# HGRN scores of a two-layer decoder: one array per block size, and the four heads scored in one stretch

## The reference, cut to what matters

```python
# hq, hf, hi: (256, 4 heads, 128) slices of h @ w_in
log_f = log(lb + (1 - lb) * sigmoid(hf));  k = (1 - lb) * sigmoid(-hf);  q = silu(hq)
b = cumsum(log_f over t)
scores[t, s] = sum_d q[t, d] * exp(b[t, d] - b[s, d]) * k[s, d]   for s <= t, else 0
o = scores @ hi * 128 ** -0.5
```

## Time and profile before

| | |
|---|---|
| median of 3 runs | 1288.95 us (1288.56 to 1290.48) |
| the profiled execution | 1287.09 us, of it 1285.1 us span |
| busy: PE, PEld, DVE, ACT, POOL | 993.1, 433.0, 243.0, 153.8, 12.6 us |
| chain that ended last | DMA 48%, PE 42%, SP's queue 4%, DVE 3% |
| mean granted TensorE clock | 0.872 of 2.4 GHz |

### The profile page before, as it was taken

One profiled execution on the slowest core, in us unless ns is written; L12 is line 12 of the kernel. 1 busy time (PEld: TensorE's weight loads), 2 busy tenths in 40 slices (PEclk: granted clock), 3 DMA queues, 4 the chain that ended last, 5 costly groups with the idle time before them and its releaser, 6 DMA issues.

```text
span 1285.1 us, 12164 instructions
## 1 busy us (share of the span) xinstructions
PE 993.1 (77%) x5148; PEld 433.0 (34%) x5148; DVE 243.0 (19%) x668; ACT 153.8 (12%) x320; POOL 12.6 (1%) x12
## 2 busy tenths in 40 slices
PE   5999998986767776766759987997776867767765
PEld 5657645421212121212227544542212312121211
DVE  3410225111101000101030564331101101000101
ACT  3523311100000000000021222110000000000000
POOL 0000001000000000000000000100000000000000
PEclk9988899987879878878789998998877878778878
DMA  7963067899999999999997413869999999999995
GB/s 248 302 248 131 14 279 296 341 429 427 428 429 426 429 426 429 427 428 428 417 392 255 149 69 148 340 280 430 427 428 427 428 427 428 427 429 426 429 421 218
DMA packets 62150, 448.53 MB, mean 349 GB/s; under 512 B 13072, under 2 KB 13328, under 8 KB 39568
## 3 DMA queue, kind: packets, MB, share of 16 engines
q1 hardware_dynamic: 62096, 447.73, 84.5%
HBM read 446.66 MB, written 1.05 MB: 348 GB/s over the span
## 4 chain that ended last, share of the span: by engine, by line
DMA 48%; PE 42%; SPq 4%; DVE 3%; ACT 1%; issue 1%; DVEq 0%; ACTq 0%
PE psum L519 17%; DMA ring<-in_w_up 14%; PE psum L741 11%; DMA ring<-in_w_down 10%; DMA wide<-in_w_gate 10%; DMA wide<-in_w_down 9%; DMA ring<-in_w_gate 5%; PE psum L783 5%; PE psum L736 2%; SPq L384 2%; SPq L328 1%; PE psum L475 1%; PE psum L836 1%; PE psum L482 1%; PE psum L838 1%
## 5 line engine op out<-in xcount | busy, mean ns | idle before, releaser
L519 PE MATMUL psum<-ring,mixed 128*32 128x512 f32 x1664 | 406.5, 714 | 123.8 <-DMA ring<-in_w_up 54.2
L519 PE MATMUL psum<-wide,mixed 128*32 128x512 f32 x1408 | 401.4, 710 | 108.8 <-DMA wide<-in_w_gate 62.4
L519 PEld LDWEIGHTS psum<-ring,mixed 128*32 128x32 f32 x1664 | 93.0, 128 | 328.1 <-issue 162.0
L519 PEld LDWEIGHTS psum<-wide,mixed 128*32 128x32 f32 x1408 | 88.6, 127 | 274.1 <-issue 123.2
L741 PE MATMUL psum<-ring,wide 128*128 128x512 f32 x320 | 145.5, 613 | 0.6 <-DMA ring<-in_w_in_ab 0.6
L741 PEld LDWEIGHTS psum<-ring,wide 128*128 128x128 f32 x320 | 62.3, 198 | 76.9 <-issue 75.8
L623 DVE TENSOR_TENSOR mixed<-psum,sig 128x512 f32<-128x512 f32 x16 | 16.9, 1056 | 277.9 <-PE psum L519 277.9
L482 PE MATMUL psum<-y_sb,spread 128*128 128x512 f32 x144 | 66.6, 605 | 1.6 <-DVE y_sb L628 1.6
L475 PE MATMUL psum<-sel,h 128*128 128x128 f32 x520 | 64.4, 283 | 3.5 <-DVE sel L596 3.5
L475 PEld LDWEIGHTS psum<-sel,h 128*128 128x128 f32 x520 | 61.0, 196 | 17.1 <-issue 13.4
L783 PE MATMUL psum<-ring,wide 128*128 128x512 f32 x128 | 58.7, 618 | 6.1 <-ACT wide L712 3.5
(11 more groups left out here) (238 smaller groups left out, 529.9 us busy)
## 6 DMA issues: line engine op xcount, KB each, us to landing
ring<-in_w_down SPq DMA_DIRECT2D x38, 2048.0 KB, 35.1
ring<-in_w_up SPq DMA_DIRECT2D x36, 2048.0 KB, 37.7
wide<-in_w_gate SPq DMA_DIRECT2D x34, 2048.0 KB, 36.6
ring<-in_w_gate SPq DMA_DIRECT2D x30, 2048.0 KB, 30.9
wide<-in_w_up SPq DMA_DIRECT2D x28, 2048.0 KB, 28.5
wide<-in_w_down SPq DMA_DIRECT2D x26, 2048.0 KB, 34.7
ring<-in_w_in_ab SPq DMA_DIRECT2D x8, 2048.0 KB, 16.6
ring<-in_w_in_cd SPq DMA_DIRECT2D x6, 2048.0 KB, 21.4
```

Of the source, the lines that this page charges most:

```text
L519: mm = pe.matmul(psum[slots, out + n, :], inp[:, c, slots], slot(layer, unit)[:, at + 512 * n:at + 512 * (n + 1)], start=c == 0, stop=c == ...
```

## The change

Per head, the score matrix is now made in five parts. The **near part** covers pairs within one block of 16: queries and keys referred to the middle of their own block, two matmuls of 128 x 128 (one for each half of the sequence; what lies outside the diagonal blocks is overwritten, or masked). Then for each **block size** 16, 32, 64, 128 one array `x_level` holds in its even blocks the keys and in its odd blocks the queries, both referred to the border between the two. One matmul per pair of blocks gives their rectangle: 8, 4, 2 and 1 matmuls with 16, 32, 64 and 128 stationary and moving columns. That is 17 matmuls a head.

ACT makes the factors with six exponentials of 128 x 1024 for all heads at once, in place of 96 short ones, and no longer takes the log of the keys. DVE makes the differences (eight subtractions of 128 x 512) and the products (two of 128 x 1024, eight of 128 x 512). POOL's two memsets go. As no array is reused, all four heads are scored behind projection 3. The masks of HGRN come before the second rotation, and the router's scaling, with its wait for the small tables, comes behind all masks. The two tables of constants get a semaphore of their own; the order of SP's DMAs stays. The new arrays lie in `h`, `wide` and `y_sb`.

```diff
             def scores_hgrn(hd):
-                pe.wait_ge(S["qe_ready"], 1)
-                pe.wait_ge(S["ke_ready"], hd + 1)
+                pe.wait_ge(S["near_ready"], 1)
                 bank = next_scores()
-                for i in range(NSUB):
-                    q = q2T[:, hd, i * SUB:(i + 1) * SUB]
-                    mm = pe.matmul(psum[:, bank, i * SUB:(i + 1) * SUB], ke0[:, i, :], q, start=True, stop=True)
...
+                for lo in range(0, SEQ, P):
+                    pe.matmul(psum[:, bank, at(lo):at(lo) + P], near_k[:, hd, lo:lo + P], near_q[:, hd, lo:lo + P],
+                              start=True, stop=True, skip_group_check=True)
+                pe.wait_ge(S["levels_ready"], len(LEVELS))
+                for width, x_level in reversed(list(zip(LEVELS, levels))):
+                    for lo in range(0, SEQ, 2 * width):
+                        mid = lo + width
+                        cols = at(mid) if width < P else P
+                        mm = pe.matmul(psum[lo % P:lo % P + width, bank, cols:cols + width], x_level[:, hd, lo:mid],
+                                       x_level[:, hd, mid:mid + width], start=True, stop=True, skip_group_check=True)
...
             for n in range(4):
                 project(0, n)
-            scores_hgrn(0)
+            for hd in range(HEADS):
+                scores_hgrn(hd)
             pe.wait_ge(S["roped"], 1)
             turn_roped(0)
             project(0, 4)
-            scores_hgrn(1)
...
             project(0, 5)
-            scores_hgrn(2)
...
-            scores_hgrn(3)
             project(0, 6)
...
             nc.scalar.activation(tmp, tmp, ACT.Ln).then_inc(S["f_log"], 1)
-            nc.scalar.activation(flat(k2T), flat(k2T), ACT.Ln).then_inc(S["f_log"], 1)
+            act.wait_ge(S["mid_in"], 1)
+            nc.scalar.activation(flat(near_k), tmp, ACT.Exp, scale=-1.0)
+            nc.scalar.activation(flat(near_q), tmp, ACT.Exp).then_inc(S["mid_exp"], 1)
+            for i, x_level in enumerate(levels):
+                act.wait_ge(S["level_in"], i + 1)
+                nc.scalar.activation(flat(x_level), flat(x_level), ACT.Exp).then_inc(S["level_exp"], 1)
             wait_projected(act, 2)
             nc.scalar.activation(flat(q2T), flat(proj(1)), ACT.Sigmoid).then_inc(S["q_sig"], 1)
...
-            dve.wait_ge(S["small_landed"], 16 * N_SMALL)
+            dve.wait_ge(S["consts_landed"], 32)
...
+            for width, x_level in zip(LEVELS, levels):
+                keys, queries = sides(cumf, width)
+                key_part, query_part = sides(x_level, width)
+                border = keys[:, :, width - 1].unsqueeze(2).broadcast_to([P, HEADS * SEQ // (2 * width), width])
+                V.tensor_tensor(key_part, border, keys, ALU.subtract)
+                V.tensor_tensor(query_part, queries, border, ALU.subtract).then_inc(S["level_in"], 1)
             dve.wait_ge(S["q_sig"], 1)
             and_wait(dve, V.tensor_tensor(flat(q2T), flat(proj(1)), flat(q2T), ALU.mult), proj_used[1], 1)
             dve.wait_ge(S["mid_exp"], 1)
+            V.tensor_tensor(flat(near_k), flat(near_k), flat(k2T), ALU.mult)
+            V.tensor_tensor(flat(near_q), flat(near_q), flat(q2T), ALU.mult).then_inc(S["near_ready"], 1)
+            for i, (width, x_level) in enumerate(zip(LEVELS, levels)):
+                dve.wait_ge(S["level_exp"], i + 1)
+                for dst, src in zip(sides(x_level, width), (sides(k2T, width)[0], sides(q2T, width)[1])):
+                    r = V.tensor_tensor(dst, dst, src, ALU.mult)
+                r.then_inc(S["levels_ready"], 1)
```

More of the change, by code:

```diff
@@ L35 @@
 NSUB = SEQ // SUB
+LEVELS = (16, 32, 64, 128)
 N_GROUPS = 4
@@ L46 @@
 KEPT_CONSTS = FIRST_CONSTS + 2 * P + SEQ + 32 + N_EXPERTS
-N_SMALL = 21
+N_SMALL = 19
 RING = 6
@@ L68 @@
 F_FLOOR = math.exp(-10.0)
-K_FLOOR = 1e-18
 SCALE = HD ** -0.5
@@ L182, in build @@
         st2 = part("mix", HEADS * TRI, "p (h n) -> p h n", h=HEADS)
-        ke0 = h[:, :, :, :].rearrange("p a b s -> p (a b) s")
-        ke1 = part("mix", NSUB // 2 * P, "p (i s) -> p i s", s=P)
+        by_head = lambda a: a.rearrange("p (h t) -> p h t", h=HEADS)
+        h_halves = h[:, :, :, :].rearrange("p a b s -> p a (b s)")
+        levels = [by_head(h_halves[:, 0, :]), by_head(h_halves[:, 1, :])]
+        levels += [part("mix", 1024, "p (h t) -> p h t", h=HEADS) for _ in range(2)]
+        near_q = part("last", 1024, "p (h t) -> p h t", h=HEADS)
         LAYER1_CONSTS = where["strict"][0]
@@ L206, in build @@
         y_sb = sb("y_sb", [P, D])[:, :]
+        near_k = by_head(y_sb)
         rt = sb("rt", [P, 512])[:, :]
@@ L223, in build @@
         over_i = sb("over_i", [P, 2], I32)
-        names = ["small_landed", "x_landed", "first_landed", "pos_landed", "lb_landed", "masks_landed", "gain_landed", "gain_used", "unit_used", "stored",
-                 "act_turn", "dve_turn", "rope_args", "rope_ready", "zeroed", "pos_ready",
+        names = ["small_landed", "x_landed", "first_landed", "pos_landed", "lb_landed", "masks_landed", "consts_landed", "gain_landed", "gain_used", "unit_used", "stored",
+                 "act_turn", "dve_turn", "rope_args", "rope_ready", "pos_ready",
                  "squares", "normed", "h_turned", "hT_ready", "lb_in", "lb_exp",
-                 "f_sig", "keys_log", "f_ready", "f_log", "cum_ready", "q_sig", "mid_in", "mid_exp", "qe_ready",
-                 "ke_ready", "scores_done", "st_ready", "pv_done", "sq_out", "out_used",
+                 "f_sig", "f_ready", "f_log", "cum_ready", "q_sig", "mid_in", "mid_exp", "level_in", "level_exp", "near_ready",
+                 "levels_ready", "scores_done", "st_ready", "pv_done", "sq_out", "out_used",
                  "roped", "turned", "turned_sb", "val_ready", "gate_sig", "gated", "mix_turned", "mixT_ready",
@@ L830, in scores_hgrn, with at @@
             def scores_hgrn(hd):
-                pe.wait_ge(S["qe_ready"], 1)
-                pe.wait_ge(S["ke_ready"], hd + 1)
+                pe.wait_ge(S["near_ready"], 1)
                 bank = next_scores()
-                for i in range(NSUB):
-                    q = q2T[:, hd, i * SUB:(i + 1) * SUB]
-                    mm = pe.matmul(psum[:, bank, i * SUB:(i + 1) * SUB], ke0[:, i, :], q, start=True, stop=True)
-                    if i >= NSUB // 2:
-                        mm = pe.matmul(psum[:, bank, SEQ - P + i * SUB:SEQ - P + (i + 1) * SUB], ke1[:, i - NSUB // 2, :], q,
-                                       start=True, stop=True)
+                def at(t):
+                    return t if t < P else t + SEQ - P
+                for lo in range(0, SEQ, P):
[8 more added lines that the diff above has]
+                                       x_level[:, hd, mid:mid + width], start=True, stop=True, skip_group_check=True)
                 mm.then_inc(S["scores_done"], 1)
@@ L1428, in _ @@
             rope_ret(2, 0)
-            mask(0, st2[:, 0, :], const("causal_scale"))
+            for hd in range(HEADS):
+                mask(hd, st2[:, hd, :], const("causal_scale"))
             rope_ret(3, GROUP_W)
-            mask(1, st2[:, 1, :], const("causal_scale"))
-            mask(2, st2[:, 2, :], const("causal_scale"))
             for hd in range(HEADS):
@@ L1435, in _ @@
                     dve.wait_ge(S["pv_done"], hd - 1)
-                mask(3 + hd, st[:, hd % 2, :], decay(hd))
-            mask(7, st2[:, 3, :], const("causal_scale"))
+                mask(HEADS + hd, st[:, hd % 2, :], decay(hd))
+            dve.wait_ge(S["small_landed"], 16 * N_SMALL)
+            for l in range(2):
+                V.tensor_tensor(rw[:, l], rw[:, l], gcol[:, l, :].unsqueeze(2).broadcast_to([P, KC, 36]),
+                                ALU.mult).then_inc(S["router_ready"], 1)
             gated_norm(0, 6, 0)
```

44 lines of the change are left out of this document (10 added, 34 removed).

## The result

| | before | after |
|---|---|---|
| median | 1289.37 us (4 runs) | 1259.05 us (4 runs, 1257.58 to 1260.38) |
| the profiled execution | 1287.09 us, span 1285.1 | 1259.15 us, span 1257.4 |
| busy: PE, PEld, DVE, ACT | 993.1, 433.0, 243.0, 153.8 us | 969.1, 409.6, 251.5, 132.4 us |
| start of projection 7 | 160.4 us | 132.4 us |

The ratio of the times is 0.9766, 95% interval 0.975 to 0.9781: 30.3 us less by the medians, 27.9 by the profiled executions. Of the 8.8 us between forecast and result, 6.8 are scores and clock; the rest is how the medians stand to the profiled executions.

The account below looks back on a forecast made before the run. PE bounds the mixer; 41.4 + 1.8 + 5.8 + 2.7 + 11.0 (scores) + 2.0 (clock) = 64.7 us for 85.9, 21.2 less, so 1265.9, plus 1.9 to the median: 1267.8 us, range 1259.5 to 1277.5.

Parts of the forecast that it names:

- the price of a narrow instruction: New HGRN scores: 28 matmuls a head of 64, 32 or 16 columns at 0.053 us each, 1.5 us a head.
- the changes of width: New scores: switching weights between 128, 64 and 32 columns costs some 0.2 us each, 0.6 us a head.
- the spell of the clock that was expected in the new stretch: One fall to 1.2 GHz from the middle of the new scoring stretch on, costing 2 us, between 0 and 3.4.
- four spells of the clock: Before the change, each of four scorings brings 6.8 us at 1.2 GHz, costing 3.4 us each, 13.6 us together.
- the account of 85.9 us: Mixer from first scoring to projection 7 before the change: work of 72.2 us plus clock spells makes 85.8, against 85.9 traced.
- The two other prices: Minimum gaps between matmuls: 25 ns, or 62 ns with software decoding, giving scores of 8.2 or 11.9 us for four heads.
- the router's rows: Profile rows of the router's 36-column matmuls: clock 1.00, then 0.60 soon behind; read as thin column use losing the clock.
- A: Rival: clock holds and narrow matmuls cost near 0.03 us each; scores 8.4 us, no spell, 1263.1 us; chance 0.33.
- B: Rival: narrow matmuls cost as much as wide; scores 17.0 us, one to two spells, 1275 to 1278.5 us; chance 0.17.
- C: Rival: narrow loads and matmuls don't overlap; slower kernel from 0.26 us per narrow instruction, 1296.7 us at 0.3; chance 0.03.
- D: Rival: the following expert stream doesn't move with the mixer, so the time stays within 0.2% of before; chance 0.02.
- Covers: Claims that other engines' work hides behind PE: factors with 13.9 us to spare; masks, second rotation and router's scaling cost nothing.

Follow-up runs that it names:

- the kernel before with its columns filled: Kernel before the change, each of its 24 scoring matmuls a head streaming 128 query columns instead of 16; scores not right; 1277.86 us.
- wide weights: Changed kernel with every narrow matmul loading 128 stationary columns instead of 64, 32 or 16, same moving columns; scores not right; 1281.86 us.

## Why the prediction was wrong, point by point

Two steps failed, both terms of the sum: the price of a narrow instruction (0.053 us taken, some 0.016 measured, 4.8 us with the small error of the changes of width) and the spell of the clock that was expected in the new stretch (2.0 us taken, none measured).

**What bounds.** Right. PE was the bound, four spells of the clock cost 13.6 us (12.4 came back when only they were removed), the account of 85.9 us closed, and in the change a microsecond of the mixer was one at the end (in the kernel before with its columns filled, 9.2 of 12.4 came out).

**Narrow matmuls: the step that failed and cost most.** I took 0.053 us for each of 28, 1.5 us a head, between a bound of columns alone and one of full weight loads. Measured: the 24 smallest are 0.014 us each, and all 28 some 0.45 us a head: 1.58 less 0.64 for the wide ones and 0.48 for three changes of width. The row that should have decided was in the prediction: the 32-column load, shorter than the 128-column one by 0.08 us, just what 96 columns of load cost at 0.107 for 128. I drew from it "below the upper end", where it said "columns count". The lower bound itself was not a bound, because neighbours overlap when their results go to different partitions. The two other prices that the prediction set beside this term, 25 and 62 ns an instruction, are both above what was measured (14 ns, and 10 in a long burst). Four heads: 6.2 us in place of 11.0, **4.8 us**.

**Changes of width.** Right in kind and size: 0.6 us a head taken, some 0.5 measured.

**The clock: the other step that failed.** I expected one spell, at 2 us, because half of the columns' time seemed little. There was none: **2.0 us**. This error leaned on the first. With a head of 1.58 us, 1.28 us of column time is four fifths and not half. It leaned also on a reading of the router's rows that they don't bear. The stretch between the two shown there, still at 1.00, has PE busy for 0.41 us only:

```profile
831.00:832.00 1.00, 0.41 (x4) 0.30 (x3) 0.97 (x2) 0.00 (x0) 0.00 (x0) 1.00 0.92 393
```

The matmuls of 36 columns ran at 1.00 to their end, then PE stood idle for 0.86 us waiting for DVE, until 832.27 us; by the 0.60 of the next stretch the clock fell at about 832.2, in that pause. Whether the thin matmuls or the idle time brought the fall, the rows don't say. And the price of a spell was wrong in the other direction: with wide weights the clock was at 0.50 for over 20 us, to the end of the scores and into projection 4, and not for 6.8.

**Sum.** With the two terms put right the sum is 57.9 us for 85.9, 28.0 less, and the profiled executions differ by 27.9. The forecast would have been 1261.0 us, inside the range. To reach the medians I had added the 1.9 us by which the profiled execution of before lay below its median; that of the change lies at its own. This is scatter between executions, and it took the result the last half microsecond out of the range.

**Rivals.** A (clock holds, narrow matmuls cheap) is what happened, with 1263.1 us given for it; it should have been the forecast, and even its 0.03 us was twice too much. B is close to the case with wide weights, which took 1281.86 us where B's upper end is 1278.5: its loads were priced rightly, the clock too low. Nor did 16 columns cost what sixty would, 0.050 us by 0.107 for 128. C's instruction costs 0.032 us where all results go to one place. D did not occur.

**Covers.** All held: factors, masks (no idle PE between heads), second rotation, router's scaling, SP's order. Retention's one wait for a mask stayed (the mask of 0.57 us is on the chain at 133.72 us before and at 114.46 after), and the stretch took the 5.8 us that the prediction gave it.

**Range.** Its lower end, 1259.5 us, was about what the bound of columns alone gives without a spell (5.9 and 2.0 us below the forecast, 1259.9). The scores came within 1.1 us of that bound. The range had no room left for a median that stands to its profiled execution otherwise than before's did, and that scatter is as large as 2 us.

## What to carry to other kernels

Price a small float32 instruction by the columns that it loads and the columns that it streams, the larger of the two: here 0.107 us for 128 of either. Take this as a rough guide below 64 columns: those of 16 and 32 took 10 to 14 ns where neighbours' results went to different partitions, and 32 ns where they didn't, and columns alone (18 ns on average) give neither. Add 0.16 us for each change of the weights' width. A matmul that loads 128 columns to stream 16 was bad twice here: it paid for the load, and with it TensorE's clock was lost for itself and for the first of the dense work behind it. Before arguing over where to place such a stretch, load no more columns than it needs. And before blaming a kind of instruction for a fall of the clock, look whether the engine stood idle just before it.

## What the runs showed of the hardware

- Being busy with weight loads did not keep TensorE's clock at 2.4 GHz: with 16 columns streamed for each load of 128 it fell to 1.2 GHz in all four scorings of before, PEld busy all the time; with the same loads and 128 columns streamed it stayed at 1.00 throughout.
- With wide weights the clock stayed at 0.50 in all of the 18 us from 80 to 98 us, and for some 5 us more; before, a fall lasted 6.8 us. This is one execution.
- Narrow matmuls whose results go to different partitions overlap: 14 ns an instruction in bursts of 24 and 10 ns in one of 192, against 32 ns in one place. At clock 0.50 they took 15 ns in a burst of 128, so they did not double.
- A change of the weights' width between 128, 64 and 32 columns cost 0.16 us.
- With 768 more of them TensorE paused five times for 1 to 3 us with no releaser in the trace, 128 or 256 PE instructions apart, so the run came to 25 ns each; the cause is open.
